# The neighbour differences of the values and one cleared row, moved from GpSimd to VectorE in a two-block mixer kernel

## The chip, the cores and the metric

The kernel runs on one core of a Trainium2 chip. The metric is the device time of one execution in microseconds (us). A core has a matrix engine (TensorE, PE in the profile, with its weight loads listed apart as PEld), VectorE (DVE), ScalarE (ACT), GpSimd (POOL) and SyncE (SP, which here only starts transfers). Each engine works through its own list of instructions in order, and the lists are tied together by semaphores.

## What is computed

The reference is a stack of three sequence mixers over 512 tokens of width 1024: a gated delta rule (A), a "stick-breaking" attention (B), and a mix of a Fourier transform with dilated window attention (C). The change lies in B, whose attention is, cut to what matters:

```python
mask = s_idx[None, :] < t_idx[:, None]
log_keep = jnp.where(mask, jax.nn.log_sigmoid(-logits), 0.0)
after = jnp.sum(log_keep, axis=-1, keepdims=True) - jnp.cumsum(log_keep, axis=-1)
wts = jnp.where(mask, jnp.exp(jax.nn.log_sigmoid(logits) + after), 0.0)
outs.append(jnp.einsum("bhts,bhsd->bhtd", wts, vb))
```

The kernel doesn't form `wts` itself. A scan along the keys gives sums that are turned and multiplied with the differences of neighbouring rows of the values, V[s] - V[s-1], in place of V. So ahead of that attention each row of the values has the row before it subtracted, and for the first row of all that neighbour is a row of zeros.

## The kernel before, in words

All matrix products with weights are done in 33 dense blocks of 512 columns (`blocks`), each in two halves s = 0, 1. A float32 weight half of 128x2048 elements is loaded into `raw`, and split into two parts so that a product is three products of parts: ScalarE writes the high part `whi` (line 784), GpSimd subtracts it from `raw` and writes the low part `wlo` (`split_lo`, line 610). TensorE waits for `lo_ready` of a half, and takes 24 matmuls of 512 columns for each of four tiles of a block (line 2074). SyncE starts the load of the next half when `lo_ready` says that `raw` is free.

The order of every engine is written by hand. Around the change it is:

- Block VB+1 (the second half of the values' columns, activations `hk`), then QB and QB+1 (queries), then ZB and ZB+1 (gates), with activations `hB`. Then the 24 rounds of the attention, in which TensorE makes scores, ScalarE the sigmoids `kept` and `taken` (lines 1199 and 1204), VectorE the scans (line 1804), TensorE turns them (line 2695) and multiplies them with `Vb` (line 2712).
- ScalarE evacuates the values into `Vb` (lines 1164 and 1148 of the profile).
- SyncE shifts `Vb` down by one row into `v_down` with four transfers, which lie behind the loads of QB+1 in its queue (lines 590 to 593).
- GpSimd does the splits of these blocks one after the other. Behind the splits of VB+1 it waits for the last tile of VB+1 (`dense_full`), and clears the row `v_down[0:1, 0, :]` (line 710). Behind the splits of ZB it waits for the clearing and the four transfers, and makes `Vb = Vb - v_down` in four instructions of 128x1024 (line 715), each of which counts `v_diff` up.
- VectorE in that time makes `hB_lo` (line 1449), copies the queries out of PSUM (line 1758) and applies their norm, which is the last thing it does ahead of the scans: `gained`, line 1768, eight instructions of 128x512 that multiply by a gain and by the root that ScalarE wrote into one of the two halves of `rbuf` (`root_pair`, lines 810 to 816). The second pair of roots of a block waits until the first pair of norms has read `rbuf`.
- ScalarE, behind the last pair of roots, loads a table and evacuates the tiles of ZB with SiLU (line 1182), and only when the first is out is the first bank free for TensorE's block ZB+1.
- ScalarE waits for all of `v_diff` ahead of the first `kept`, since `kept` lies where `v_down` was:

```python
if r == 0:
    act.wait_ge(v_diff, 1 + NT)
A(of_round(kept, r), logits(r), ACT.Sigmoid, scale=-1.0).then_inc(kept_done, 1)
```

Of the kernel before, what the change touches and what calls it, by code (L numbers as in the profile page):

```python
# [11 lines left out]
ALU = mybir.AluOpType  # L12
# [7 lines left out]
NT = T // 128  # L20
# [84 lines left out]
def mixer_stack(nc, x, c, norm_g, w_ada, b_ada, w_in_a, conv_w_a, a_log_a, dt_bias_a, o_gain_a, w_out_a,  # L105
# [3 lines left out]
    with ctx:  # L109
        def sb(name, shape, dt=F32, scope=None):  # L110
            return (scope or ctx).enter_context(nc.sbuf_tensor(name, shape, dt))

        def sem(name):
            return ctx.enter_context(nc.semaphore(name))
# [96 lines left out]
        with ExitStack() as B:  # L211
# [4 lines left out]
            with ExitStack() as s2:  # L216
                v_down = sb("v_down", [128, NT, D], F32, s2)
# [15 lines left out]
            Vb = sb("Vb", [128, NT, D], F32, B)  # L233
# [105 lines left out]
        def early(u):  # L339

            return (ada_a if u % EARLY < 2 else ada_b)[:, u % 2 + 2 * (u // EARLY), :].rearrange("p (k n) -> p k n", k=KD)

        halves = [sum(kind == "t" for _, _, kind in blocks[:d]) for d in range(len(blocks))]

        def unit_used(eng, d, s):
# [47 lines left out]
        hi_ready, lo_ready, half_done, dense_full = (sem(n) for n in ("hi_ready", "lo_ready", "half_done", "dense_full"))  # L393
# [213 lines left out]
        def _(pool):  # L607
            def split_lo(d, s):
                pool.wait_ge(hi_ready, 2 * d + s + 1)
                pool.tensor_tensor(wlo[:, s, :], raw[:, s, :], whi[:, s, :].bitcast(F32),  # L610
                                   ALU.subtract).then_inc(lo_ready, 1)
# [93 lines left out]
            for d in range(D_OUTA + 1, D_OUTB):  # L705
                for s in range(1 if d in own_parts else 2):
                    split_lo(d, s)
                if d == D_VB + 1:
                    pool.wait_ge(dense_full, 4 * (D_VB + 2))
                    pool.memset(v_down[0:1, 0, :], 0.0).then_inc(v_diff, 1)  # L710
                if d == D_ZB:
                    pool.wait_ge(v_diff, 1)
                    pool.wait_ge(v_shifted, 64)
                    for j in range(NT):
                        pool.tensor_tensor(Vb[:, j, :], Vb[:, j, :], v_down[:, j, :], ALU.subtract).then_inc(v_diff, 1)
            split_lo(D_OUTB, 0)
            split_lo(D_OUTB, 1)
            for d in range(D_OUTB + 1, len(blocks)):
# [655 lines left out]
        def _(dve):  # L1374
            STT, TT, copy = dve.scalar_tensor_tensor, dve.tensor_tensor, dve.tensor_copy
# [384 lines left out]
            def raw_rows(d, dst, classes=False):  # L1760
                for j in range(4):
                    raw_row(d, j, dst(j), classes)

            def gained(g, n, dst, gain):
                for j in range(4):
                    dve.wait_ge(r_ready, g + j + 1)
                    dve.wait_ge(kq_done, n + j + 1)
                    STT(dst(j), dst(j), gain(j), rbuf[:, (g + j) % 2, :], ALU.mult, ALU.mult).then_inc(kqn_done, 1)
# [7 lines left out]
            for b in range(2):  # L1776
                raw_rows(D_QB + b, lambda j: qTb[:, 4 * b + j, :])
                gained(G_QB + 4 * b, 8 + 4 * b, lambda j: qTb[:, 4 * b + j, :], lambda j: qcol[:, 0:1])


            def yb(kt):
# [1254 lines left out]
```

## Time and profile before

| what | value |
|---|---|
| time before, median of 3 runs | 1182.68 us (1181.45 to 1183.99) |
| the profiled execution, its own time | 1180.23 us |
| its span in the trace | 1178.2 us |
| TensorE busy | 1123.5 us, 95% |
| ScalarE busy | 520.1 us, 44% |
| VectorE busy | 496.7 us, 42% |
| GpSimd busy | 381.6 us, 32% |
| DMA, mean over the span | 101 GB/s |

The span runs from the first to the last instruction of the core, and the execution's own time is 2.0 us longer. Busy is the time in which an engine had an instruction under way, so a matmul at half the clock is busy for twice as long and the share doesn't show it. The column PEclk of the views by stretch is the TensorE clock that was granted, as a share of 2.4 GHz: 1.00 is 2.4 GHz and 0.50 is 1.2 GHz. Times of single instructions count from the start of the span.

### The profile page before, as it was taken

How to read it: one execution, taken by the hardware profiler on the slowest of the kernel's cores; microseconds unless marked ns; L12 is line 12 of the kernel's file. 1: busy time of each engine (PE TensorE's matmuls, PEld its weight loads, DVE VectorE, ACT ScalarE, POOL GpSimd, SP SyncE). 2: the span in 40 equal slices, each digit the busy share in tenths (PEclk: the TensorE clock that was granted, in tenths of full speed). 3: DMA queues.
4: the chain of work that ended last, by engine and by line, in shares of the span. 5: the costliest groups of instructions: out<-in, count | busy, mean ns of one | idle time of the engine just before them, and what ended most of it. 6: DMA issues, size and time to landing. Idle time of an engine off the chain costs nothing.

```text
span 1178.2 us, 21348 instructions
## 1 busy us (share of the span) xinstructions
PE 1123.5 (95%) x8978; PEld 883.7 (75%) x8978; DVE 496.7 (42%) x889; ACT 520.1 (44%) x911; POOL 381.6 (32%) x153
## 2 busy tenths in 40 slices
PE   5999999999989999998998999999999999999998
PEld 3688886777668889776776667888877777778767
DVE  3575553453323356242131884653203342231563
ACT  5232326653326534452345884343234433743540
POOL 0134432233236341433463101324343133433260
PEclk7899999999999999998999999999999999999999
DMA  9822331185651122234322100322232421324201
GB/s 312 260 72 82 96 107 54 54 287 183 218 179 38 37 95 64 92 99 126 98 76 104 37 1 1 107 90 87 76 107 72 116 81 37 107 72 154 99 1 72
DMA packets 103006, 119.37 MB, mean 101 GB/s; under 512 B 4679, under 2 KB 89207, under 8 KB 102791
## 3 DMA queue, kind: packets, MB, share of 16 engines
q1 hardware_dynamic: 99054, 115.08, 30.4%
q10 hardware_dynamic: 3864, 3.01, 0.9%
q8 instruction: 68, 1.11, 0.4%
q14 instruction: 20, 0.16, 0.0%
HBM read 110.75 MB, written 2.10 MB: 96 GB/s over the span
## 4 chain that ended last, share of the span: by engine, by line
PE 82%; ACT 7%; DVE 5%; issue 4%; DMA 1%; SPq 1%; ACTq 0%; POOL 0%; DVEq 0%
PE ps L2074 42%; PE ps L2867 4%; PE ps L2120 2%; PE ps L2462 2%; PE ps L2215 2%; PE ps L2677 2%; PE ps L2712 2%; PE ps L2158 1%; PE ps L2695 1%; PE ps L2291 1%; PE ps L2833 1%; PE ps L2489 1%; PE ps L2238 1%; PE ps L2820 1%; DMA ada_a<-in_w_ada_dram 1%
## 5 line engine op out<-in xcount | busy, mean ns | idle before, releaser
L610 POOL TENSOR_TENSOR wlo<-raw,whi 128x2048 fp32r<-128x2048 f32 x53 | 245.4, 4632 | 514.2 <-ACT whi L784 501.8
L784 ACT ACTIVATE whi<-raw 128x2048 fp32r<-128x2048 f32 x52 | 99.3, 1911 | 202.0 <-PE ps L2074 160.9
L616 POOL TENSOR_TENSOR wlo<-raw,whi 128x2048 fp32r<-128x2048 f32 x10 | 46.4, 4643 | 111.6 <-ACT whi L873 62.9
L1804 DVE TENSOR_TENSOR_SCAN taken<-kept,taken 128x255 f32<-128x255 f32 (+2 forms) x64 | 51.2, 853 | 33.2 <-ACT taken L1204 33.1
L1294 ACT ACTIVATE p<-sc,nmx 128x256 f32<-128x256 f32 x64 | 32.0, 501 | 45.9 <-PE ps L2820 44.7
L1901 DVE CUSTOM_DVE_ANT_0 sc<-ps,biast 128x256 f32<-128x256 f32 (+1 forms) x64 | 22.5, 393 | 65.8 <-PE ps L2809 36.8
L873 ACT ACTIVATE whi<-raw 128x2048 fp32r<-128x2048 f32 x11 | 21.1, 1917 | 62.7 <-PE ps L2074 62.7
L2074 PE MATMUL ps<-hC_hi,whi 128*128 128x512 f32 x184 | 46.9, 397 | 0.8 <-POOL wlo L610 0.8
L2074 PE MATMUL ps<-hC_lo,whi 128*128 128x512 f32 x184 | 45.5, 390 | 0.0
L2074 PE MATMUL ps<-hC_hi,wlo 128*128 128x512 f32 x184 | 45.4, 389 | 0.0
L2074 PEld LDWEIGHTS ps<-hC_hi,whi 128*128 128x128 f32 x184 | 33.7, 188 | 14.8 <-issue 6.4
L2074 PE MATMUL ps<-hB_hi,whi 128*128 128x512 f32 x120 | 33.3, 424 | 8.9 <-issue 5.6
L2074 PEld LDWEIGHTS ps<-hC_lo,whi 128*128 128x128 f32 x184 | 34.5, 188 | 7.4
L2074 PEld LDWEIGHTS ps<-hC_hi,wlo 128*128 128x128 f32 x184 | 34.5, 188 | 7.2
L2074 PE MATMUL ps<-hA_lo,whi 128*128 128x512 f32 x160 | 39.5, 389 | 0.0
L2074 PE MATMUL ps<-hA_hi,wlo 128*128 128x512 f32 x160 | 39.5, 389 | 0.0
L2074 PE MATMUL ps<-hA_hi,whi 128*128 128x512 f32 x160 | 39.5, 389 | 0.0
L1472 DVE SCALAR_TENSOR_TENSOR work<-ps,cols,work 128x511 f32<-128x511 f32 (+1 forms) x48 | 36.0, 749 | 6.1 <-DVE work L1469 0.2
L2074 PEld LDWEIGHTS ps<-hB_hi,whi 128*128 128x128 f32 x120 | 23.8, 203 | 17.8 <-issue 12.9
L1592 DVE COPY_PREDICATED yib<-cs,ps 128x256 f32<-128x256 int32 x20 | 10.0, 501 | 59.9 <-PE ps L2462 59.9
L625 POOL COPY yib<-cs 128x512 f32<-128x512 f32 x20 | 12.6, 630 | 70.1 <-PE ps L2490 70.1
L2074 PEld LDWEIGHTS ps<-hA_hi,wlo 128*128 128x128 f32 x160 | 30.0, 188 | 6.2
(506 smaller groups left out, 2696.5 us busy)
## 6 DMA issues: line engine op xcount, KB each, us to landing
raw<-in_w_in_dram SPq DMA_DIRECT2D x24, 1024.0 KB, 5.2
raw<-in_w_in_a_dram SPq DMA_DIRECT2D x16, 1024.0 KB, 5.6
raw<-in_w_ada_dram SPq DMA_DIRECT2D x8, 1024.0 KB, 5.2
late_w<-in_w_ada_dram SPq DMA_DIRECT2D x8, 1024.0 KB, 5.5
raw<-in_w_kv_dram SPq DMA_DIRECT2D x8, 1024.0 KB, 5.3
raw<-in_w_in_b_dram SPq DMA_DIRECT2D x8, 1024.0 KB, 5.4
ada_a<-in_w_ada_dram SPq DMA_DIRECT2D x4, 1024.0 KB, 11.2
ada_b<-in_w_ada_dram SPq DMA_DIRECT2D x4, 1024.0 KB, 11.9
```

The costliest lines, as they stand in the source:

```text
L610: pool.tensor_tensor(wlo[:, s, :], raw[:, s, :], whi[:, s, :].bitcast(F32), ALU.subtract).then_inc(lo_ready, 1)
L616: pool.tensor_tensor(wlo[:, s, :], raw[:, s, :], whi[:, s, :].bitcast(F32), ALU.subtract).then_inc(lo_ready, 1)
L784: A(whi[:, s, :], raw[:, s, :], ACT.Copy).then_inc(hi_ready, 1)
L1294: A(p2[:, n % 2, 256 * e:256 * e + 256], sc2[:, n % 2, 256 * e:256 * e + 256], ACT.Exp, scale=-1.0, bias=nmx[:, grp, t, 2 * hp + e:2 * hp ...
L1472: STT(y[:, n:], src[:, 0:T - n], tap(3 - n), y[:, n:], ALU.mult, ALU.add).then_inc(conv_step, 1)
L1804: last = dve.tensor_tensor_scan(taken[:, r % 3, keys], kept[:, r % 3, keys], taken[:, r % 3, keys], 0.0, ALU.mult, ALU.add)
L2074: last = mm(out, l[a], r[b], start=start and at == 0, stop=stop and at == n - 1)
L2120: last = mm(dense[m][:, cols], w[:, k, 128 * (m % 2):128 * (m % 2) + 128], x[:, k, cols], start=half == 0 and q == 0, stop=stop and q == 2 ...
L2215: last = mm(modrow(2 * EARLY)[32 * (k % 4):32 * (k % 4) + 32, :], cactz[:, k, 23 - n:55 - n], late_src(a, s)[:, k, :], start=n == 0 and k ...
L2462: last = mm(block64(0, s, i, 1 - n), ntm[side(n), (2 * p + s) % 4, i, :], xin[side(n), (2 * p + s) % 4, i, :], start=True, stop=True)
L2677: mm(logits(r)[:, e, at:at + 128 * i + 128], qTb[side(e), kt, 128 * i:128 * i + 128], kTb[side(e), kt, 0:128 * i + 128], start=at == 0, st ...
L2867: last = mm(dense[2 * s + m], w[:, k, 128 * m:128 * m + 128], x[:, k, :], start=q == 0, stop=q == 23)
```

## The change

The clearing of the row and the four subtractions are taken out of GpSimd's list and put into VectorE's, behind the last norm of the queries and ahead of the first scan. They wait for the same semaphores as before, and count `v_diff` as before. Transfers, matmuls and ScalarE's list stay as they are.

```diff
@@ GpSimd
             for d in range(D_OUTA + 1, D_OUTB):
                 for s in range(1 if d in own_parts else 2):
                     split_lo(d, s)
-                if d == D_VB + 1:
-                    pool.wait_ge(dense_full, 4 * (D_VB + 2))
-                    pool.memset(v_down[0:1, 0, :], 0.0).then_inc(v_diff, 1)
-                if d == D_ZB:
-                    pool.wait_ge(v_diff, 1)
-                    pool.wait_ge(v_shifted, 64)
-                    for j in range(NT):
-                        pool.tensor_tensor(Vb[:, j, :], Vb[:, j, :], v_down[:, j, :], ALU.subtract).then_inc(v_diff, 1)
             split_lo(D_OUTB, 0)
@@ VectorE
             for b in range(2):
                 raw_rows(D_QB + b, lambda j: qTb[:, 4 * b + j, :])
                 gained(G_QB + 4 * b, 8 + 4 * b, lambda j: qTb[:, 4 * b + j, :], lambda j: qcol[:, 0:1])
+            dve.wait_ge(dense_full, 4 * (D_VB + 2))
+            dve.memset(v_down[0:1, 0, :], 0.0).then_inc(v_diff, 1)
+            dve.wait_ge(v_diff, 1)
+            dve.wait_ge(v_shifted, 64)
+            for j in range(NT):
+                TT(Vb[:, j, :], Vb[:, j, :], v_down[:, j, :], ALU.subtract).then_inc(v_diff, 1)
```

GpSimd's list before, from the end of part A on. The ten splits ahead of the clearing are those of the blocks OUTA (second half) to VB+1, the six behind it those of QB, QB+1 and ZB:

```order
L701 TENSOR_TENSOR osb<-osb,zs 128x512 [waits os_done] x2
L610 TENSOR_TENSOR wlo<-raw,whi 128x2048 [waits hi_ready] x10
L710 MEMSET v_down 1x1024 [waits dense_full]
L610 TENSOR_TENSOR wlo<-raw,whi 128x2048 [waits hi_ready] x6
L715 TENSOR_TENSOR Vb<-Vb,v_down 128x1024 [waits v_shifted,v_diff]
L715 TENSOR_TENSOR Vb<-Vb,v_down 128x1024 x3
L610 TENSOR_TENSOR wlo<-raw,whi 128x2048 [waits hi_ready] x31
```

The same place with the change, where 10, 6 and 31 splits have become 47 in a row and none of them stands behind a wait for `dense_full` or `v_shifted`:

```order
L701 TENSOR_TENSOR osb<-osb,zs 128x512 [waits os_done] x2
L610 TENSOR_TENSOR wlo<-raw,whi 128x2048 [waits hi_ready] x47
L717 CAST picks<-picks_raw 16x1024 [waits v_moved0,v_moved1,fc_loaded,gate_done]
L730 TENSOR_TENSOR qA<-qA,ga 128x512 [waits n_done] x4
L725 TENSOR_TENSOR qB<-qB,ga 128x512 [waits n_done] x2
```

VectorE's list with the change, from the queries of QB to the first scans (in the order's names the scan reads SCALAR_TENSOR_TENSOR):

```order
L1750 COPY qTb<-ps 128x512 [waits dense_full] x4
L1760 SCALAR_TENSOR_TENSOR qTb<-qTb,qcol,rbuf 128x512 [waits kq_done,r_ready] x4
L1750 COPY qTb<-ps 128x512 [waits dense_full] x4
L1760 SCALAR_TENSOR_TENSOR qTb<-qTb,qcol,rbuf 128x512 [waits kq_done,r_ready] x4
L1772 MEMSET v_down 1x1024 [waits dense_full]
L1776 TENSOR_TENSOR Vb<-Vb,v_down 128x1024 [waits v_shifted,v_diff]
L1776 TENSOR_TENSOR Vb<-Vb,v_down 128x1024 x3
L1802 SCALAR_TENSOR_TENSOR taken<-kept,taken 128x511 [waits taken_done,kept_done]
L1802 SCALAR_TENSOR_TENSOR taken<-kept,taken 128x511
```

Before, the norms (line 1768 there) were followed at once by the scans (line 1804 there); the five instructions between them are new.

## Rows read from the trace of the kernel before

**Rows 1.** Who TensorE waited for: in total, times, longest (us)
```profile
PE ps L2074 <- issue: 5.6, 1, 5.6
...
PE ps L2074 <- ACT zsT L1182: 3.3, 1, 3.3
```
**Rows 2.** Timeline of VectorE, ScalarE, GpSimd, first place: start us, us, engine, instruction, [idle before]
```profile
534.80 1.63 DVE L1449 SCALAR_TENSOR_TENSOR hB_lo<-tmpu,mods,hB_hi 128x512 fp32r<-128x512 f32 x2
...
535.55 1.90 ACT L784 ACTIVATE whi<-raw 128x2048 fp32r<-128x2048 f32 x1
...
540.96 0.94 POOL L710 MEMSET v_down<- 1x1024 f32 x1 [14.67 <-PE ps L2074]
541.87 4.49 POOL L610 TENSOR_TENSOR wlo<-raw,whi 128x2048 fp32r<-128x2048 f32 x1
```
**Rows 3.** Timeline of TensorE at the same place
```profile
546.46 3.75 PE L2074 MATMUL ps<-hB_hi,whi 128*128 128x512 f32 x8 [5.56 <-issue]
550.01 2.78 PE L2074 MATMUL ps<-hB_lo,whi 128*128 128x512 f32 x8
552.63 1.99 PE L2074 MATMUL ps<-hB_hi,wlo 128*128 128x512 f32 x8
554.45 1.98 PE L2074 MATMUL ps<-hB_hi,whi 128*128 128x512 f32 x8
```
**Rows 4.** By stretch, TensorE alone: stretch, its us, PE busy, PEclk, DMA share, GB/s
```profile
544.00:546.00 2.00, 0.00 (x0) 0.71 0.00 0
```
**Rows 5.** Timeline of ScalarE, GpSimd and VectorE, second place
```profile
606.19 1.91 ACT L784 ACTIVATE whi<-raw 128x2048 fp32r<-128x2048 f32 x1 [7.44 <-PE ps L2074]
...
602.40 9.47 POOL L715 TENSOR_TENSOR Vb<-Vb,v_down 128x1024 f32<-128x1024 f32 x4
611.82 5.04 POOL L610 TENSOR_TENSOR wlo<-raw,whi 128x2048 fp32r<-128x2048 f32 x1
...
610.78 1.63 DVE L1768 SCALAR_TENSOR_TENSOR qTb<-qTb,qcol,rbuf 128x512 f32<-128x512 f32 x1 [14.35 <-ACT rbuf L814]
...
612.34 5.08 DVE L1768 SCALAR_TENSOR_TENSOR qTb<-qTb,qcol,rbuf 128x512 f32<-128x512 f32 x1
...
620.80 1.28 ACT L1182 ACT_TABLE_LOAD   x1
```
**Rows 6.** Timeline of TensorE at the second place
```profile
622.83 3.30 PE L2074 MATMUL ps<-hB_hi,whi 128*128 128x512 f32 x8 [3.34 <-ACT zsT L1182]
625.93 2.39 PE L2074 MATMUL ps<-hB_lo,whi 128*128 128x512 f32 x8
628.16 1.98 PE L2074 MATMUL ps<-hB_hi,wlo 128*128 128x512 f32 x8
```
**Rows 7.** Timeline of GpSimd and VectorE, the same pair of norms one block earlier
```profile
583.90 4.63 POOL L610 TENSOR_TENSOR wlo<-raw,whi 128x2048 fp32r<-128x2048 f32 x1 [6.23 <-ACT whi L784]
...
586.50 3.25 DVE L1768 SCALAR_TENSOR_TENSOR qTb<-qTb,qcol,rbuf 128x512 f32<-128x512 f32 x2 [14.84 <-ACT rbuf L814]
```
**Rows 8.** VectorE's groups by line and shape: count | busy us, mean ns | idle before
```profile
L1689 DVE TENSOR_TENSOR wk_lo<-raw,wk_hi 128x1024 fp32r<-128x1024 f32 x2 | 2.4, 1220 | 0.0
...
L1837 DVE MEMSET wbd<- 128x1024 f32 x1 | 0.9, 912 | 0.2 <-issue 0.2
```
**Rows 9.** Timeline of GpSimd and ScalarE: the next split, and the first sigmoid of the attention
```profile
626.03 4.62 POOL L610 TENSOR_TENSOR wlo<-raw,whi 128x2048 fp32r<-128x2048 f32 x1 [9.16 <-ACT whi L784]
...
643.17 1.03 ACT L1199 ACTIVATE kept<-ps 128x1024 f32<-128x1024 f32 x1 [0.23 <-PE ps L2681]
```
**Rows 10.** By stretch, TensorE alone, around two short stalls of part A
```profile
321.00:322.00 1.00, 0.03 (x3) 1.00 0.00 0
323.00:324.00 1.00, 1.00 (x24) 0.50 0.37 74
337.00:338.00 1.00, 0.00 (x0) 1.00 1.09 361
...
340.00:341.00 1.00, 1.00 (x64) 1.00 0.10 34
```

## The prediction, made before the result was known

> **What bounds the kernel now.** I read the share of busy time first: TensorE is busy for 95% of the span, so the question is what GpSimd's five instructions do to TensorE's few pauses. The view of who TensorE waited for gives the two longest that lie near them [rows 1]: one of 5.6 us whose releaser the profile does not name ("issue"), and one of 3.3 us behind the SiLU that frees a bank (line 1182). The timelines of the other engines at these two places say who is really behind each, and both times it is an instruction that the change takes off GpSimd.
>
> First place, the start of block QB. TensorE is done with VB+1 at 540.90 (its restart at 546.46 less the 5.56 us of idling in the row) [rows 3]. The high part of QB's first weights was ready at 535.55 + 1.90 = 537.45, and hB_lo, which QB also needs, at 536.43 [rows 2]. Only the low part was missing. GpSimd had been idle for 14.67 us, but in its list the clearing of the row stood ahead of the split, with a wait for the end of VB+1: it started at 540.96, and the split at 541.87 [rows 2]. The split took 4.49 us to the start of the next one, and TensorE went on 0.1 us later. So the pause is a row of zeros that waits for TensorE and makes TensorE wait in turn.
>
> Second place, the start of block ZB+1. TensorE's pause ends with the SiLU, behind a table load at 620.80, behind ScalarE's second pair of roots, behind the first pair of the queries' norms. That pair ran from 610.78 to 612.34 + 5.08 = 617.42 [rows 5], where two instructions of VectorE of the same size and kind took 1.63 us together at 534.80 [rows 2]. The first of the two ended when GpSimd's fourth subtraction was done, and the second when the split behind it was done (611.82 + 5.04 = 616.86) [rows 5]: an instruction of VectorE with two inputs in SBUF and one of GpSimd do not run at the same time, and each waits for the whole of the other. GpSimd came to that split late, since it did the subtractions from 602.40 to 611.87, though ScalarE had its input ready at 606.19 + 1.91 = 608.10 [rows 5].
>
> Both pauses cost more than their length. The granted clock was 0.71 on average in the stretch 544 to 546 [rows 4], that is, it fell from 2.4 to 1.2 GHz while TensorE idled, and the first groups of eight matmuls then took 3.55 and 2.62 us from start to start, against 1.82 us for the next [rows 3]. At the second place they took 3.10 and 2.23 us [rows 6].
>
> **The change part by part.** *The clearing leaves GpSimd.* The split of QB can start at 537.45 and the 0.06 us that GpSimd took behind its releaser at the clearing (540.90 to 540.96 [rows 2, 3]), so at 537.51. With its 4.49 us and the 0.1 us to TensorE, the matmuls start at 537.51 + 4.49 + 0.10 = 542.10 in place of 546.46: **4.36 us**. A pause of 542.10 - 540.90 = 1.20 us stays. If the clock holds over it, the slow groups go too: (3.55 + 2.62) - 2 x 1.82 = **2.53 us** [rows 3]. Does it hold? The trace has a pause of about 2 us behind which the clock fell (busy 0.03 from 321 to 322, clock 0.50 from 323 on) and one behind which it did not (nothing done from 337 to 338, clock 1.00 at 340) [rows 10]. 1.20 us is shorter than both, so I take the whole term; the bounds are nothing and 2.53 us, and the first is a rival below.
>
> *The subtractions leave GpSimd.* The split of ZB+1's first half starts at 608.10 + 0.06 = 608.16 in place of 611.82, and ends at 608.16 + 4.63 = 612.79. The norms ask at 610.78 still and find GpSimd reading. That is just how the same pair fared one block earlier: the split started at 583.90, the pair at 586.50, and the pair was done at 586.50 + 3.25 = 589.75, 5.85 us behind the split's start [rows 7]. So now it is done at 608.16 + 5.85 = 614.01, where it was 617.42: 3.41 us. Everything behind it, roots, table load and SiLU, is a chain without slack up to TensorE's restart, which could come at 622.83 - 3.41 = 619.42. TensorE's last group ends at 622.83 - 3.34 = 619.49, so the pause goes as a whole and no more than it can be won: **3.34 us**. Without a pause the clock has no reason to fall: (3.10 + 2.23) - 2 x 1.82 = **1.69 us** [rows 6]. Bounds: nothing, if the pair is blocked as long as before, and 5.03 us.
>
> *The five instructions on VectorE.* A subtraction of this shape takes 1.22 us there, a clearing at most 0.91 us [rows 8]: 0.91 + 4 x 1.22 = 5.8 us. VectorE's last two norms were done by 620.80 + 1.63 = 622.4 at the latest, since the last roots stand ahead of the table load [rows 2, 5]. Now that is 622.4 - 3.4 = 619.0, and the subtractions are done by 624.8 (all in the times of the trace before, with the first place's gain left aside). They hide under ZB+1's matmuls: VectorE has nothing to do until the first scan, and the first who wants them is ScalarE's first sigmoid, at 643.17 - 5.03 = 638.1 [rows 9], 13 us later. What lay beyond these 13 us would be paid in full. Their other contact is GpSimd's next split, at 626.03 before [rows 9] and at 622.6 now. It meets the subtractions, and ends at 622.6 + 4.6 = 627.2 if it goes first and at 624.8 + 4.6 = 629.4 if all of them do. TensorE needs it after the six groups of ZB+1's first half, at 619.49 + 6 x 1.82 = 630.4. So nothing is lost, with 1.0 us to spare in the worst order. The four transfers into v_down keep their places in SyncE's queue and are done long before either reader.
>
> The Trainium skill speaks against this change in "Perfetto Trace Analysis", section "Optimizing Scalar/DVE Operations": the two engines share a read port, so moving operations between them might not help. The rows agree that they block each other, but not that it makes no difference here: the 9.47 us on GpSimd become 4.9 us on VectorE, at a time when neither list is waited for. By the skill's rule the second place would give nothing, and the sum would be the first place's alone; that is rival C.
>
> **The sum.** 4.36 + 2.53 + 3.34 + 1.69 = 11.92 us. The profiled execution's own time of 1180.23 would become 1168.3. It lay 2.45 us under the median of the three runs, and the terms are differences, so they are taken off the median: 1182.68 - 11.9 = **1170.8 us**. The rest of the program moves up as it stands, since every split, load and evacuation there is released by TensorE.
>
> **The rivals.** *B, the clock still falls at one place.* The pause of 1.20 us may be enough, together with what else TensorE lacks around it; the pair of pauses in [rows 10] shows that pauses of one length can go either way. That gives back 1.69 to 2.53 us: 1172.5 to 1173.3. In its favour is that the fall at 323 came behind a pause of only 2 us. Against it: 1.20 us is little over half of that. The Trainium skill, "TensorE: Matmul & The Clock Gate", section "Part 1: The HAM clock gate (the "warmup" mystery)", says that the clock is set by how busy the array was of late; [rows 10] agree.
>
> *C, the port moves the stall instead of ending it.* The norms are blocked as long as before, by a split that starts at another moment or by a second one. Then only the first place pays: 1182.68 - 6.89 = 1175.8. Against it stands the pair of [rows 7], which met the same split and lost 1.8 us, not 5.
>
> *D, the first pause is not the clearing's.* TensorE's row names no releaser. If something else held QB until near 546, only the second place pays: 1182.68 - 5.03 = 1177.7. Against it: the 0.1 us from the split's end to the restart.
>
> *E, the sigmoids wait for the differences, and it gets slower.* The place is ScalarE's wait on v_diff in round 0. If each subtraction waited for a split of 4.6 us, the last would end at 619.0 + 0.9 + 4 x (1.2 + 4.6) = 643.1, 5.0 us late, which still leaves a gain of 6.9. To be slower it must end over 11.9 us behind 638.1, that is after 650, or 7.5 us for each subtraction. The longest that any norm was held up in [rows 5] is 5.08 us, so this needs something that the trace does not have.
>
> **How the numbers follow.** The forecast has 0.70, B 0.14, C 0.06, D 0.05, and no change at all, where both gains are lost on the way to the end, 0.02. E, and whatever else makes it slower, has 0.03. The forecast's own spread is the 1.3 us by which the three runs lie about their median and about 1 us for the terms. So the range goes from 1168.6 up through B to 1174.6, which leaves out C, D, E and a little of both tails, under 2 in 10. A measurement of this kernel can tell about 0.2% (2.4 us) from no change. Forecast, B, C and D are all beyond that: faster 0.95, same 0.02, slower 0.03.
>
> **What would show it.** TensorE's pause before QB is 1.2 us and the one before ZB+1 is gone; groups of eight matmuls start every 1.82 us at both places, with the clock at 1.00; GpSimd's split of QB starts 0.1 us behind ScalarE's high part; the first pair of the last norms takes about 3.2 us, not 6.6; the subtractions take 4.9 us on VectorE and end 13 us ahead of the first sigmoid. I am wrong if a pause of 3 us or more stands at either place, if the clock drops there, or if TensorE waits for the split of ZB+1's second half or for the first sigmoid.

## The result, and the profile after

| what | before | after |
|---|---|---|
| median (lowest to highest) | 1182.81 us (1181.45 to 1183.99), 4 runs | 1167.89 us (1166.64 to 1170.30), 4 runs |
| ratio to before, 95% interval | | 0.9889 [0.9872, 0.9906] |
| span of the profiled execution | 1178.2 us | 1165.2 us |

The change makes the kernel 1.1% faster: 13.1 us by the ratio, 11 to 15 us by its interval, and 14.9 us between the medians. The prediction was 1170.8 us in a range of 1168.6 to 1174.6, so the measured median lies 2.9 us under the forecast and 0.7 us below the range's lower end (the ratio, applied to the 1182.68 us it started from, gives 1169.6 us, inside the range). Measured a second time (below) it was 1169.61 us, 13.5 us under before. Where the difference lies is seen in the trace, and there the changed stretch gives 11.7 us.

The page of the changed kernel, its first part (busy us, share of the span, instructions):

```profile
span 1165.2 us, 21348 instructions
...
PE 1118.7 (96%) x8978; PEld 881.2 (76%) x8978; DVE 504.2 (43%) x894; ACT 520.0 (45%) x911; POOL 371.0 (32%) x148
```

GpSimd's busy time fell by 10.6 us and VectorE's rose by 7.5 us. TensorE has the same matmuls and is busy for 4.8 us less; 4.1 us of that are the matmuls at the two places below, which before ran at 1.2 GHz.

Who TensorE waited for, after (in total, times, longest), against [rows 1]:

```profile
PE ps L2072 <- issue: 1.3, 1, 1.3
...
PE ps L2675 <- ACT zsT L1179: 0.8, 1, 0.8
```

The pause of 5.6 us is down to 1.3 us, and the one of 3.3 us is gone from the list. The 0.8 us ahead of the attention's first scores are behind another SiLU (the last that ScalarE makes before the scores), and the kernel before has them too.

The first place after, GpSimd and ScalarE, then TensorE, against [rows 2, 3]:

```profile
534.28 1.90 ACT L776 ACTIVATE whi<-raw 128x2048 fp32r<-128x2048 f32 x1
...
536.26 4.59 POOL L610 TENSOR_TENSOR wlo<-raw,whi 128x2048 fp32r<-128x2048 f32 x1 [11.23 <-ACT whi L776]
...
540.96 2.06 PE L2072 MATMUL ps<-hB_hi,whi 128*128 128x512 f32 x8 [1.32 <-issue]
542.86 1.98 PE L2072 MATMUL ps<-hB_lo,whi 128*128 128x512 f32 x8
544.67 1.98 PE L2072 MATMUL ps<-hB_hi,wlo 128*128 128x512 f32 x8
```

What released GpSimd's split is now ScalarE's high part, 0.08 us ahead of it (534.28 + 1.90 = 536.18), and not TensorE. The next groups of eight matmuls start after 1.90 and 1.81 us, where it was 3.55 and 2.62 us.

The second place after, GpSimd, VectorE, ScalarE, then TensorE, against [rows 5, 6]:

```profile
600.21 4.63 POOL L610 TENSOR_TENSOR wlo<-raw,whi 128x2048 fp32r<-128x2048 f32 x1 [5.76 <-ACT whi L776]
614.68 4.76 POOL L610 TENSOR_TENSOR wlo<-raw,whi 128x2048 fp32r<-128x2048 f32 x1 [9.84 <-ACT whi L776]
...
602.81 3.25 DVE L1760 SCALAR_TENSOR_TENSOR qTb<-qTb,qcol,rbuf 128x512 f32<-128x512 f32 x2 [14.35 <-ACT rbuf L806]
608.94 1.42 DVE L1760 SCALAR_TENSOR_TENSOR qTb<-qTb,qcol,rbuf 128x512 f32<-128x512 f32 x2 [2.88 <-ACT rbuf L806]
610.50 0.91 DVE L1772 MEMSET v_down<- 1x1024 f32 x1
611.45 9.08 DVE L1776 TENSOR_TENSOR Vb<-Vb,v_down 128x1024 f32<-128x1024 f32 x4
...
630.22 1.03 ACT L1191 ACTIVATE kept<-ps 128x1024 f32<-128x1024 f32 x1 [0.23 <-PE ps L2679]
...
609.55 1.97 PE L2072 MATMUL ps<-hB_hi,wlo 128*128 128x512 f32 x8
611.48 2.06 PE L2072 MATMUL ps<-hB_hi,whi 128*128 128x512 f32 x8
613.38 1.98 PE L2072 MATMUL ps<-hB_lo,whi 128*128 128x512 f32 x8
```

The first pair of norms takes 3.25 us in place of 6.63, and TensorE goes from one block to the next in 1.93 us, against 1.81 us inside a block. The subtractions, 9.08 us and not 4.9, met the split at 614.68, and still ended at 620.5, 9.7 us ahead of the first sigmoid.

By stretch, TensorE alone (stretch, its us, PE busy, PEclk, DMA share, GB/s), the clock stays up, against [rows 4]:

```profile
540.00:542.00 2.00, 1.04 (x5) 1.00 0.04 4
542.00:544.00 2.00, 2.00 (x11) 1.00 0.87 260
544.00:546.00 2.00, 2.00 (x10) 1.00 0.78 269
```

**A measure that depends less on the run.** The first 540 us of the traces here differ by up to 6.3 us though nothing in them was changed (VB+1 ends at 540.90 before, at 539.64 after, and between 537.4 and 543.7 in the experiments). So the experiments are compared by the stretch from the end of VB+1 to the first scores of the attention. Before, it is 641.79 - 540.90 = 100.89 us; after, 628.83 - 539.64 = 89.19 us. The difference is 11.70 us. The stretch still varies by 0.7 us with the clock, as the run with the subtractions alone will show.

### The profile page after: what moved, and what is told of

Read it like the earlier page. It is cut to its first block, busy times and chain, and to the rows that moved or that the text cites. A ratio compares the mean times of both kernels' runs of the same rounds, so it can differ in the third digit from the quotient of the medians.

```text
span 1165.2 us, 21348 instructions
## 1 busy us (share of the span) xinstructions
PE 1118.7 (96%) x8978; PEld 881.2 (76%) x8978; DVE 504.2 (43%) x894; ACT 520.0 (45%) x911; POOL 371.0 (32%) x148
## 4 chain that ended last, share of the span: by engine, by line
PE 83%; ACT 6%; DVE 4%; issue 3%; DMA 1%; ACTq 0%; SPq 0%; POOL 0%; DVEq 0%
PE ps L2072 43%; PE ps L2865 4%; PE ps L2118 2%; PE ps L2460 2%; PE ps L2213 2%; PE ps L2675 2%; PE ps L2710 2%; PE ps L2156 1%; PE ps L2693 1%; PE ps L2236 1%; PE ps L2289 1%; PE ps L2831 1%; PE ps L2487 1%; PE ps L2818 1%; DMA ada_a<-in_w_ada_dram 1%
## 5 line engine op out<-in xcount | busy, mean ns | idle before, releaser
L2072 PEld LDWEIGHTS ps<-hA_hi,whi 128*128 128x128 f32 x160 | 30.0, 188 | 6.2
L2072 PEld LDWEIGHTS ps<-hA_lo,whi 128*128 128x128 f32 x160 | 30.0, 188 | 6.2
```

What stands on the lines that cost most here:

```text
L2072: last = mm(out, l[a], r[b], start=start and at == 0, stop=stop and at == n - 1)
```

## The experiments

My theory: two pauses of TensorE, each with a fall of its clock behind it. The first is GpSimd's wait for the end of VB+1, which stood ahead of a split that was ready to go. The second is the subtractions, which made the next split late, so that it met the pair of norms. The rivals are those of the prediction, and beside them a question that it left open: was it the engine or the order? All runs give medians against the runs of the kernel before on the same chip.

| kernel | median, us | before there, us | ratio [95% interval] | stretch, us |
|---|---|---|---|---|
| clearing alone | 1175.17 | 1181.80 | 0.9951 [0.9932, 0.9969] | 94.24 |
| subtractions alone | 1176.51 | 1181.80 | 0.9952 [0.9927, 0.9976] | 95.17 |
| GpSimd, reordered | 1173.91 | 1181.80 | 0.9935 [0.9917, 0.9952] | 93.02 |
| change, wait kept | 1175.42 | 1181.80 | 0.9953 [0.9938, 0.9967] | 95.28 |
| change again | 1169.61 | 1183.13 | 0.9889 [0.9868, 0.9910] | 89.22 |
| change, QB's split on VectorE | 1169.06 | 1183.13 | 0.9878 [0.9857, 0.9900] | 87.63 |
| GpSimd, later still | 1168.31 | 1183.13 | 0.9879 [0.9853, 0.9905] | 89.22 |
| change, subtractions late | 1185.12 | 1183.13 | 1.0021 [1.0002, 1.0040] | 89.22, and 15.6 more by round 6 |
| split past the wait | 1170.12 | 1181.83 | 0.9914 [0.9887, 0.9941] | 87.63 |
| subtractions earlier | 1169.48 | 1181.83 | 0.9916 [0.9885, 0.9948] | 89.23 |

### One half of the change alone

The clearing alone goes to VectorE, ahead of the copies of QB:

```diff
-                if d == D_VB + 1:
-                    pool.wait_ge(dense_full, 4 * (D_VB + 2))
-                    pool.memset(v_down[0:1, 0, :], 0.0).then_inc(v_diff, 1)
@@ VectorE, behind the norm for hB
+            dve.wait_ge(dense_full, 4 * (D_VB + 2))
+            dve.memset(v_down[0:1, 0, :], 0.0).then_inc(v_diff, 1)
             for b in range(2):
                 raw_rows(D_QB + b, lambda j: qTb[:, 4 * b + j, :])
```

> Only the clearing goes to VectorE, ahead of the queries' copies of QB, where VectorE idles; the subtractions stay on GpSimd at their old place. Theory (two separate stalls, each with its clock): the first place's terms alone, 4.4 us of pause and 2.5 us of clock, so 6.9 us under the kernel before: about 1176. The pause before QB is 1.2 to 1.3 us, the one before ZB+1 stays at 3.3 us and the pair of norms at 6.6 us. Rival (the first pause is not the clearing's): no gain here.

Measured: 6.6 us under before, and 6.65 us in the stretch. The first place is as after the change, and the second as before, in TensorE's timeline:

```profile
540.66 2.08 PE L2073 MATMUL ps<-hB_hi,whi 128*128 128x512 f32 x8 [1.32 <-issue]
...
614.61 3.64 PE L2073 MATMUL ps<-hB_hi,whi 128*128 128x512 f32 x8 [3.34 <-ACT zsT L1179]
618.09 2.02 PE L2073 MATMUL ps<-hB_lo,whi 128*128 128x512 f32 x8
```

The subtractions alone go to VectorE:

```diff
-                if d == D_ZB:
-                    pool.wait_ge(v_diff, 1)
-                    pool.wait_ge(v_shifted, 64)
-                    for j in range(NT):
-                        pool.tensor_tensor(Vb[:, j, :], Vb[:, j, :], v_down[:, j, :], ALU.subtract).then_inc(v_diff, 1)
@@ VectorE, behind the last norm
+            dve.wait_ge(v_diff, 1)
+            dve.wait_ge(v_shifted, 64)
+            for j in range(NT):
+                TT(Vb[:, j, :], Vb[:, j, :], v_down[:, j, :], ALU.subtract).then_inc(v_diff, 1)
```

> Only the subtractions go to VectorE, behind the last norm; the clearing stays on GpSimd with its wait. Theory: the second place's terms alone, 3.3 us of pause and 1.7 us of clock, so 5.0 us under the kernel before: about 1178. The pause before QB stays at 5.6 us, the one before ZB+1 is gone and the pair of norms takes 3.25 us. Rival (the port moves the stall): no gain here.

Measured: 5.3 us under before, and 5.72 us in the stretch. The second pause is gone and the first one stands, in TensorE's timeline:

```profile
545.74 3.75 PE L2073 MATMUL ps<-hB_hi,whi 128*128 128x512 f32 x8 [5.56 <-issue]
549.29 2.07 PE L2073 MATMUL ps<-hB_lo,whi 128*128 128x512 f32 x8
551.20 1.98 PE L2073 MATMUL ps<-hB_hi,wlo 128*128 128x512 f32 x8
```

The halves add up to 12.4 us, 0.7 us more than the change. That is the clock: behind the same pause of 5.56 us the first two groups took 3.55 + 1.91 us here and 3.55 + 2.62 us in the kernel before, since the clock came back earlier. So the pauses are fixed to 0.1 us, and the clock's share of their price varies from trace to trace.

### The wait or the clearing

The change, with one line put back on GpSimd:

```diff
+                if d == D_VB + 1:
+                    pool.wait_ge(dense_full, 4 * (D_VB + 2))
```

> The change, but GpSimd keeps its wait for the last tile of VB+1 at the place where the clearing stood. Theory (it was the wait, not the 0.94 us of clearing): the pause before QB is back to 5.6 - 0.9 = 4.7 us and the clock falls again, so 3.4 + 1.7 to 2.5 us slower than the change, 1173 to 1174. Rival (the clearing itself): within 1 us of the change.

Measured: the median 6.4 us under before, where the change had 13.5 to 14.9 us, and 6.09 us longer than the change in the stretch. TensorE's timeline:

```profile
545.48 3.75 PE L2074 MATMUL ps<-hB_hi,whi 128*128 128x512 f32 x8 [4.69 <-issue]
549.03 3.02 PE L2074 MATMUL ps<-hB_lo,whi 128*128 128x512 f32 x8
551.89 2.00 PE L2074 MATMUL ps<-hB_hi,wlo 128*128 128x512 f32 x8
```

The pause is 3.37 us longer than after the change, and the clock takes 2.7 us more. The expectation had 5.1 to 5.9 us for the two, and its median of 1173 to 1174 us was at least 1.4 us too low. A wait that costs no busy time at all costs 6 us. The clearing itself is the 0.87 us between 4.69 and 5.56.

Then the reverse: the wait and the clearing stay on GpSimd, and what stood behind them leaves. The subtractions are on VectorE, and so is the low part of QB's first half:

```diff
@@ GpSimd
                 for s in range(1 if d in own_parts else 2):
-                    split_lo(d, s)
+                    if (d, s) == (D_QB, 1):
+                        pool.wait_ge(lo_ready, 2 * D_QB + 1)
+                    if (d, s) != (D_QB, 0):
+                        split_lo(d, s)
@@ VectorE, behind the norm for hB
+            dve.wait_ge(hi_ready, 2 * D_QB + 1)
+            dve.wait_ge(lo_ready, 2 * D_QB)
+            TT(wlo[:, 0, :], raw[:, 0, :], whi[:, 0, :].bitcast(F32), ALU.subtract).then_inc(lo_ready, 1)
```

> The clearing and its wait stay on GpSimd at the old place, the subtractions go to VectorE, and VectorE also makes the low part of QB's first half. Theory (what cost time was the one split that stood behind the wait): with that split elsewhere the wait is harmless, since GpSimd's next split gets its input only about 2.4 us behind the end of VB+1. So there is no pause before QB and none before ZB+1, and it is as fast as the version with the split on VectorE and the clearing moved (87.6 us from the end of VB+1 to the first scores), 13 us under before. Rival (the wait costs by itself): a pause of 1 us or more before QB or between its halves.

Measured: 11.7 us under before, and a stretch of 87.63 us, with no pause at either place. The medians give 1.6 us less than the stretch (100.89 - 87.63 = 13.26 us) and than the 13 us expected; their interval reaches from 7.0 to 13.4 us. GpSimd's timeline:

```profile
539.75 0.94 POOL L713 MEMSET v_down<- 1x1024 f32 x1 [14.67 <-PE ps L2079]
542.27 4.64 POOL L610 TENSOR_TENSOR wlo<-raw,whi 128x2048 fp32r<-128x2048 f32 x1 [1.58 <-ACT whi L782]
```

The wait is the same 14.67 us long as in [rows 2] and costs nothing, since GpSimd is idle again for 1.58 us behind the clearing. What the wait costs is set by what is queued behind it.

### The engine or the order

All five instructions stay on GpSimd. The clearing comes behind both splits of QB, and the subtractions behind the split of ZB+1's first half:

```diff
             for d in range(D_OUTA + 1, D_OUTB):
                 for s in range(1 if d in own_parts else 2):
                     split_lo(d, s)
+                    if (d, s) == (D_ZB + 1, 0):
+                        pool.wait_ge(v_diff, 1)
+                        pool.wait_ge(v_shifted, 64)
+                        for j in range(NT):
+                            pool.tensor_tensor(Vb[:, j, :], Vb[:, j, :], v_down[:, j, :], ALU.subtract).then_inc(v_diff, 1)
+                if d == D_QB:
+                    pool.wait_ge(dense_full, 4 * (D_VB + 2))
+                    pool.memset(v_down[0:1, 0, :], 0.0).then_inc(v_diff, 1)
-                if d == D_VB + 1:
...
-                if d == D_ZB:
...
```

> All five instructions stay on GpSimd, but later in its list: the clearing behind both splits of QB, the subtractions behind the split of ZB+1's first half. Theory (order, not engine): as fast as the change, within 1 us, since the critical split no longer stands behind them; the second pair of norms will be held up by the subtractions, up to 2.4 us each, which nobody is waiting for then. Rival (what helps is that GpSimd has less to do and VectorE does it four times as fast... the engine itself): it keeps most of the time of the kernel before, 1178 or more.

Measured: 7.9 us under before, and 3.8 us longer than the change in the stretch. Neither expectation holds. (The rival's "four times as fast" is not so either: one subtraction takes 2.40 us on GpSimd and 1.22 us on VectorE.) The first place gained all of its terms, the second only a quarter: 1.25 us of pause and nothing of the clock. GpSimd's, VectorE's and TensorE's timelines:

```profile
604.30 4.63 POOL L610 TENSOR_TENSOR wlo<-raw,whi 128x2048 fp32r<-128x2048 f32 x1 [5.74 <-ACT whi L784]
608.89 10.77 POOL L712 TENSOR_TENSOR Vb<-Vb,v_down 128x1024 f32<-128x1024 f32 x4
...
606.89 5.39 DVE L1768 SCALAR_TENSOR_TENSOR qTb<-qTb,qcol,rbuf 128x512 f32<-128x512 f32 x2 [14.34 <-ACT rbuf L814]
615.16 5.05 DVE L1768 SCALAR_TENSOR_TENSOR qTb<-qTb,qcol,rbuf 128x512 f32<-128x512 f32 x2 [2.88 <-ACT rbuf L814]
...
617.70 2.49 PE L2074 MATMUL ps<-hB_hi,whi 128*128 128x512 f32 x8 [2.09 <-ACT zsT L1182]
619.99 3.22 PE L2074 MATMUL ps<-hB_lo,whi 128*128 128x512 f32 x8
```

I had looked at the second pair of norms, for which nobody waits, and forgotten that the first pair has two members. The first norm gets its turn when the split ends; then it is GpSimd's turn again, with its first subtraction, and the second norm waits for that: 5.39 us in place of 3.25. The pause of 2.09 us is that delay, and the clock fell again. So I put the subtractions one split later, behind (ZB+1, 1), with nothing else changed:

```diff
-                    if (d, s) == (D_ZB + 1, 0):
+                    if (d, s) == (D_ZB + 1, 1):
```

> All five instructions on GpSimd, the subtractions now behind both splits of ZB+1. With them behind the first split (the run before this one) the second norm of the pair met the first subtraction and 2.1 us of the pause stayed. Theory (place in the order and not the engine): here they run from about 619.3 to 629, after all four norms, and end 1 us ahead of the first sigmoid, so as fast as the change within 1 us, and no pause before ZB+1. Rival (GpSimd can't hide them anywhere): the sigmoids wait or a split comes late, 2 us or more slower than the change.

Measured: 1168.31 us, beside 1169.61 us for the change on the same chip, and the same stretch to 0.1 us. GpSimd's and ScalarE's timelines:

```profile
615.29 4.64 POOL L610 TENSOR_TENSOR wlo<-raw,whi 128x2048 fp32r<-128x2048 f32 x1 [9.83 <-ACT whi L784]
619.89 9.45 POOL L712 TENSOR_TENSOR Vb<-Vb,v_down 128x1024 f32<-128x1024 f32 x4
...
630.82 1.03 ACT L1199 ACTIVATE kept<-ps 128x1024 f32<-128x1024 f32 x1 [0.23 <-PE ps L2681]
```

The subtractions end at 629.34, 1.5 us ahead of the sigmoid. So nothing in the gain needs VectorE: a better place in GpSimd's own list gives the same. VectorE buys room (9.7 us ahead of the sigmoid in place of 1.5).

The opposite check puts the five instructions on VectorE at an earlier place, between the copies and the norms of QB+1:

```diff
             for b in range(2):
                 raw_rows(D_QB + b, lambda j: qTb[:, 4 * b + j, :])
+                if b:
+                    dve.wait_ge(dense_full, 4 * (D_VB + 2))
+                    dve.memset(v_down[0:1, 0, :], 0.0).then_inc(v_diff, 1)
+                    dve.wait_ge(v_diff, 1)
+                    dve.wait_ge(v_shifted, 64)
+                    for j in range(NT):
+                        TT(Vb[:, j, :], Vb[:, j, :], v_down[:, j, :], ALU.subtract).then_inc(v_diff, 1)
                 gained(G_QB + 4 * b, 8 + 4 * b, lambda j: qTb[:, 4 * b + j, :], lambda j: qcol[:, 0:1])
```

> The change with the clearing and the subtractions on VectorE one step earlier, between the copies and the norms of QB+1, where VectorE idles for 14 us. There they meet GpSimd's split of ZB's second half. Theory (each waits for the whole of one instruction of the other, and both have slack there): the split starts 1 us late, the subtractions take about 9 us, no pause of TensorE, within 1 us of the change. Rival (the place behind the norm matters): the split or the norms come late, a pause before ZB's second half or ZB+1, 1.5 us or more slower than the change.

Measured: 12.3 us under before, and a stretch of 89.23 us. GpSimd's and VectorE's timelines:

```profile
589.40 5.47 POOL L610 TENSOR_TENSOR wlo<-raw,whi 128x2048 fp32r<-128x2048 f32 x1 [9.25 <-ACT whi L776]
...
589.14 9.08 DVE L1776 TENSOR_TENSOR Vb<-Vb,v_down 128x1024 f32<-128x1024 f32 x4
```

The split is held up for 0.8 us and the subtractions for 4.5 us, and both had the slack. Behind the norm is not a special place.

### The price of the cover

The cover is the time between the end of the subtractions and the first instruction that waits for them. This is the change, with the row cleared 26 times over ahead of the subtractions:

```diff
-            dve.memset(v_down[0:1, 0, :], 0.0).then_inc(v_diff, 1)
-            dve.wait_ge(v_diff, 1)
+            for n in range(26):
+                if n:
+                    dve.wait_ge(v_diff, n)
+                dve.memset(v_down[0:1, 0, :], 0.0).then_inc(v_diff, 1)
+            dve.wait_ge(v_diff, 26)
@@ ScalarE
-                    act.wait_ge(v_diff, 1 + NT)
+                    act.wait_ge(v_diff, 26 + NT)
```

> The change with the clearing done 26 times over ahead of the subtractions, which makes them end at about 640.6 in place of 620.5, 10.4 us behind the moment at which the first sigmoid was ready to go (630.2). This prices the cover. By the prediction's account what lies beyond the cover is paid in full: 10.4 us slower than the change. By the trace of the change TensorE has last_gate's matmuls until 636.8 and ScalarE idles 1.4 us and more behind its first sigmoids, so some 3 us more are covered: 7 to 9 us slower, the clock's fall included. If nobody waits for the differences: within 1 us of the change.

Measured: 15.5 us slower than the change (1185.12 against 1169.61), and by its interval slower than the kernel before. Each clearing took 1.18 us from start to start with its wait, not 0.95, so the subtractions were later than planned. VectorE's, ScalarE's and TensorE's timelines:

```profile
638.69 4.63 DVE L1779 TENSOR_TENSOR Vb<-Vb,v_down 128x1024 f32<-128x1024 f32 x4
...
643.41 1.02 ACT L1191 ACTIVATE kept<-ps 128x1024 f32<-128x1024 f32 x1 [15.67 <-DVE Vb L1779]
...
645.40 1.65 PE L2678 MATMUL ps<-kTb,qTb 64*128 64x256 f32 x8 [10.81 <-ACT taken L1196]
...
654.40 1.51 PE L2696 MATMUL ps<-cs,taken 128*128 128x128 f32 x6 [2.68 <-DVE taken L1805]
```

The first scores came at 626.59. The sigmoid that follows them after 1.39 us in the changed kernel (628.83 to 630.22) came 16.82 us behind them: 15.43 us late. The scores of round 3 came 23.15 us behind the first ones, 10.00 us in the change, so 13.1 us late and 2.3 us were covered by TensorE's other work. By round 6 it was 36.61 against 21.05 us, 15.6 us late, so 2.4 us came back. In between, TensorE's clock was at 0.50 for part of the time, and it waited 2.68 us for a scan where it waits for 1.13 us in the change; how the 2.4 us divide between the two is not shown. The expectation had some 3 us covered, of which 2.3 us were seen, and at most 1.6 us lost again by the clock (9 - (10.4 - 3)), where 2.4 us came back. The two cancelled, so the prediction's "paid in full" was the better number, by luck of the sizes. The subtractions came 15.4 us late and not the 10.4 us designed, so this is one point, 15.6 us paid for 15.4 us late, and whether less lateness is paid in full too is not shown.

### The rest of the first pause, and the change once more

The change, with QB's first low part made by VectorE, is the split of the diff above without the clearing on GpSimd:

> The change, and VectorE also makes the low part of QB's first half (2.28 us in the trace, GpSimd's takes 4.6), right behind the norm for hB. What is left of the pause before QB is GpSimd's split, so theory: the low part is ready at 538.5, ahead of the end of VB+1 at 539.6, and the pause of 1.3 us is gone: 1.3 us under the change. Rival (the 1.3 us are TensorE's own, at the change of operands): no gain.

> The change itself once more, beside the runs of the kernel before on this chip. The trace of the change shows 11.7 us between the end of VB+1 and the first scores, and the medians of the first measurement stood 14.9 us apart (interval 11.1 to 15.1). Theory (the change is worth the 11.7 us of that stretch, the rest is spread of the runs): 11 to 13 us under before. Rival (something outside of the stretch gained 3 us as well): 14 to 15 us again, and the parts ahead of 540 or behind 629 shorter in this trace.

The change measured again: 13.5 us under before, 11.7 us in the stretch. Outside of the stretch its trace is 1.4 us shorter than that of before ahead of the end of VB+1 (539.54 against 540.90) and 0.5 us longer behind the first scores (536.9 against 536.4). Both are in the range of kernels that changed nothing there.

With the split on VectorE the stretch is 1.6 us shorter than with the change, and the medians (1169.06 and 1169.61, 0.6 us apart, with intervals of the ratios 0.4% wide) can't tell them apart. The expected 1.3 us show in the stretch alone. TensorE and VectorE at the first place:

```profile
540.41 1.07 PE L2078 MATMUL ps<-whi,hk_lo 128*128 128x512 f32 x4
541.31 1.98 PE L2078 MATMUL ps<-hB_hi,whi 128*128 128x512 f32 x8
...
538.06 2.29 DVE L1773 TENSOR_TENSOR wlo<-raw,whi 128x2048 fp32r<-128x2048 f32 x1 [1.06 <-ACT whi L779]
```

TensorE goes from one block into the next in 0.90 us a group of four, as inside a block. So the 1.3 us that the change leaves are GpSimd's 4.6 us for a split which VectorE does in 2.3, and not TensorE's own. In the stretch this version is the shortest together with the split past the wait; over the whole span its trace (1166.1 us) is no shorter than the two of the change (1165.2 and 1165.7 us).

## Why the prediction was right, and where it was off

- **The first pause** was to shrink from 5.56 to 1.20 us, 4.36 us: measured 1.32 us, so 4.24. GpSimd took 0.08 us behind ScalarE and not 0.06, and the split 0.1 us longer. The runs with the clearing alone and with the wait kept show it to be the wait, and rule out rival D.
- **Its clock**, 2.53 us: measured (3.55 + 2.62) - (1.90 + 1.81) = 2.46 us. Rival B did not come: behind a pause of 1.3 us the groups ran at full pace in all six traces that have it at this place (the change twice, the clearing alone, both orders on GpSimd, the subtractions earlier) and in the one with the late subtractions.
- **The second pause**, 3.34 us: measured from the last group of ZB to the first of ZB+1, 5.31 us before and 1.93 us after, so 3.38 us. **Its clock**, 1.69 us: measured 3.10 + 2.23 - (1.90 + 1.82) = 1.61 us. The pair of norms took 3.25 us, as the pair of [rows 7] had said. Rival C did not come in the change, but its mechanism is real: the reordered version on GpSimd is a case of it.
- **The sum** of 11.92 us stands against 11.70 us in the trace. The sum was right to 0.2 us; the level of the median was not, by 2.9 us in the first measurement and 1.2 us in the second. The median that the terms were taken off was sound: 1182.68 us, against 1182.81 and 1183.13 us with more runs. What was sized too small is the scatter by which a median of a few runs lies off its stretch, put at 1.3 us and about 1 us for the terms. In ten measurements (all but the late subtractions) the medians gained between 1.6 us less and 3.2 us more than the stretch did, and the first one is the highest of them. Of the 13.0 us between the two profiled spans, 1.3 us lie ahead of the end of VB+1, where no instruction was changed. Why the medians of the change stood lower than the stretch accounts for is not settled; the interval of the ratio, 11 to 15 us, has 11.7 us inside.
- **The subtractions** were said to take 4.9 us and took 9.08 us. The text had both orders of them and the split, and then gave the number without a meeting as the sign to look for. 4.63 us is what they take undisturbed (in the run with the subtractions alone). Nothing hung on it: they ended 9.7 us ahead of the sigmoid, and the split at 619.4, well ahead of its use near 622. The four transfers, which the prediction put at no cost without a row, cost nothing: in the run with the subtractions earlier, VectorE began the subtractions, which wait for them, at 589.14 and without idling, 22 us before it did in the change.
- **The rule** that I set against the change, in the Trainium skill, "Perfetto Trace Analysis", section "Optimizing Scalar/DVE Operations", says that moving work between these two engines might not help, since they share a read port. The traces show both sides of it. The engine did not matter, as the rule has it: GpSimd with the better order is as fast. And the change helped all the same, for a reason that the rule does not speak of, the place in the list.
- **The rows on the clock.** The prediction said that [rows 10] agree with the Trainium skill, "TensorE: Matmul & The Clock Gate", section "Part 1: The HAM clock gate (the "warmup" mystery)", that the clock is set by how busy the array was of late. They do so only in part: one pause there is 1.9 us long with a fall behind it, the other 2.2 us with none. That the clock held behind 1.3 us was a bet on the shorter length, and it came out in all seven traces.
- **Rival E** was priced by "what lay beyond is paid in full": 15.4 us late cost 15.6 us, at one point.

## What to carry to other kernels

An engine that is idle for most of the time can hold up the engine that bounds the kernel: look at what stands at the head of its list during the idle time, and whether something behind it is ready. A wait costs what is queued behind it, so a small item with a late condition goes behind the work that is due sooner, on whatever engine. Price a pause of TensorE with the clock behind it: here 5.6 us cost 7.3 to 8.0, and 3.3 us cost 5.0.

## What the runs showed of the hardware

VectorE's instructions with two inputs in SBUF and GpSimd's take turns one by one when both have more to do. In the reordered kernel a subtraction came between two norms; in the change the split came between the third and the fourth subtraction, and four of them took 9.08 us where they take 4.63 us alone. So behind a long instruction of the other engine an instruction can be held up again by the next. This agrees with the Trainium skill, "SBUF — State Buffer", section "Who interferes with whom", that an instruction of VectorE with two inputs in SBUF contends with one of GpSimd that reads SBUF, over ports that are locked and not shared out, and that the order of issue decides who is blocked. That the turn then passes to the other engine each time is what these traces add.

Whether the clock falls behind a pause of some 2 us is not fixed. The same pause of part A is 1.9 us long in eleven of the twelve traces; a fall followed in seven of them, the kernel before among them [rows 10], and none in the other four, such as the run with the clearing alone (by stretch, TensorE alone):

```profile
320.00:321.00 1.00, 0.00 (x0) 1.00 0.00 0
321.00:322.00 1.00, 0.38 (x6) 1.00 0.00 0
322.00:323.00 1.00, 1.00 (x33) 1.00 0.06 16
323.00:324.00 1.00, 1.00 (x27) 1.00 0.54 98
```

At the two places of the change a pause of 1.3 us was never followed by a fall (seven traces), the one of 2.09 us was, and those of 3.3 to 5.6 us were each time (five pauses in four traces).
